# Order and form of the opening work of a two-layer encoder kernel: input halves, first weights, filter layers and filter maximum

## What is computed

```python
for layer in range(2):
    x = x + 0.5 * swiglu(rms_norm(x, ffn1_norm[layer]), wg, wu, wd)      # D_FF = 2816
    h = rms_norm(x, mix_norm[layer])
    x = x + (hyena_attention_mixer(h, ...) if layer == 0 else rwkv7_bidir_mixer(h, ...))
    x = x + 0.5 * swiglu(rms_norm(x, ffn2_norm[layer]), wg2, wu2, wd2)

# hyena_filter(L), which depends on weights alone, not on x:
hf = sin(freq * (z @ f1_w + f1_b))        # z: 256 x 33, layers of 64
hf = sin(freq * (hf @ f2_w + f2_b))
hf = sin(freq * (hf @ f3_w + f3_b))
hf = hf @ f4_w                            # 64 -> 2 x 512
h_f, h_b = hf[:, :512] * window, hf[:, 512:] * window
filt = concat(h_f[:1] + h_b[:1], h_f[1:], 0, h_b[:0:-1]);  filt /= sum(|filt|)
```

## Time and profile before

| | |
|---|---|
| median of 3 executions | 1247.82 us (1247.22 to 1248.85) |
| the profiled execution, device time | 1250.58 us |
| span of its trace, first to last instruction | 1248.8 us |
| PE busy | 1204.4 us (96%) |
| DVE, ACT, POOL busy | 804.6 us (64%), 657.7 us (53%), 404.7 us (32%) |
| chain of work that ended last | PE 81%, DVE 10%, ACT 6% |
| mean granted clock of PE | 0.986 |

### The profile page before, as it was taken

The page is one execution under the profiler, slowest core; times in us unless marked ns, Lnnn a source line. Parts: engine busy times, 40 slices in busy tenths (PEclk is TensorE's granted clock), DMA queues, the critical chain, the costliest instruction groups (busy, mean ns, idle before and its releaser), DMA issues.

```text
span 1248.8 us, 27159 instructions
## 1 busy us (share of the span) xinstructions
PE 1204.4 (96%) x11086; PEld 1086.2 (87%) x11086; DVE 804.6 (64%) x1280; ACT 657.7 (53%) x1118; POOL 404.7 (32%) x218
## 2 busy tenths in 40 slices
PE   8999999988999999999999989997999999999998
PEld 5899999876989999989999979986999888899998
DVE  7655555787685555485555479758777757755554
ACT  5545444664275445474454446665666544654552
POOL 0343443321123443323434410015343412334433
PEclk9999999998999999999999989988999999999999
DMA  9355445422255445554554534411000015554552
GB/s 359 110 194 202 171 182 202 152 102 102 101 205 200 167 185 202 195 199 175 189 201 166 194 146 152 152 51 53 4 4 4 3 59 198 203 193 166 195 190 96
DMA packets 18657, 187.99 MB, mean 151 GB/s; under 512 B 2065, under 2 KB 2577, under 8 KB 3601
## 3 DMA queue, kind: packets, MB, share of 16 engines
q1 hardware_dynamic: 18576, 186.84, 41.2%
HBM read 185.78 MB, written 1.05 MB: 150 GB/s over the span
## 4 chain that ended last, share of the span: by engine, by line
PE 81%; DVE 10%; ACT 6%; issue 1%; POOL 0%; DMA 0%; SPq 0%; DVEq 0%
PE gu_bank L265 24%; PE gu_bank L267 12%; PE bank L244 7%; PE bank L246 7%; PE bank L245 7%; PE bank L1446 7%; PE gu_bank L244 3%; PE gu_bank L1446 3%; PE gu_bank L246 3%; PE gu_bank L245 3%; DVE WL L199 2%; ACT WH L187 2%; PE gu_bank L1477 2%; DVE HX L395 1%; ACT WH L193 1%
## 5 line engine op out<-in xcount | busy, mean ns | idle before, releaser
L208 POOL TENSOR_TENSOR WL<-raw,WH 128x1024 fp32r<-128x1024 f32 x96 | 328.0, 3416 | 595.5 <-ACT WH L193 573.7
L265 PE MATMUL gu_bank<-HX,WH 128*128 128x512 f32 x1408 | 504.0, 400 | 6.4 <-DVE PL L531 4.5
L267 PE MATMUL gu_bank<-HX,WL 128*128 128x256 f32 x1408 | 396.0, 281 | 0.0
L199 DVE TENSOR_TENSOR WL<-raw,WH 128x2048 fp32r<-128x2048 f32 (+1 forms) x114 | 245.1, 2150 | 130.3 <-ACT WH L187 130.3
L265 PEld LDWEIGHTS gu_bank<-HX,WH 128*128 128x128 f32 x1408 | 265.4, 188 | 70.3 <-DVE PL L531 5.1
L267 PEld LDWEIGHTS gu_bank<-HX,WL 128*128 128x128 f32 x1408 | 266.8, 190 | 0.2
L187 ACT ACTIVATE WH<-raw 128x2048 fp32r<-128x2048 f32 (+1 forms) x114 | 205.0, 1799 | 26.5 <-PE gu_bank L246 14.4
L244 PE MATMUL bank<-PH,WH 128*128 128x256 f32 (+1 forms) x720 | 201.7, 284 | 1.0 <-ACT arena L2043 0.9
L245 PE MATMUL bank<-PL,WH 128*128 128x256 f32 (+1 forms) x720 | 201.6, 283 | 0.0
L246 PE MATMUL bank<-PH,WL 128*128 128x256 f32 (+1 forms) x720 | 201.5, 283 | 0.0
L452 ACT ACTIVATE work<-gu_bank 128x512 f32<-128x512 f32 x88 | 52.5, 597 | 168.3 <-PE gu_bank L267 168.3
(11 more groups left out here) (313 smaller groups left out, 1811.5 us busy)
## 6 DMA issues: line engine op xcount, KB each, us to landing
raw<-stream_in SPq DMA_DIRECT2D x114, 1536.0 KB, 6.5
cst<-const_in SPq DMA_DIRECT2D x1, 1568.0 KB, 17.8
X<-xT_in SPq DMA_DIRECT2D x1, 1024.0 KB, 6.1
raw<-stream_in SPq DMA_DIRECT2D x1, 1024.0 KB, 8.1
arena<-hconst_in SPq DMA_DIRECT2D x2, 512.0 KB, 11.4
out<-X SPq DMA_DIRECT2D x4, 256.0 KB, 2.1
arena<-hconst_in SPq DMA_DIRECT2D x1, 768.0 KB, 14.5
arena<-fw_in SPq DMA_DIRECT2D x1, 512.0 KB, 8.9
```

Of the source, the lines that this page charges most:

```text
L199: nc.vector.tensor_tensor(WL[:, slot, :cut], raw[:, slot, :cut], WH[:, slot, :cut].bitcast(fp32), ALU.subtract).then_inc(lo_ready, 1)
L208: (eng or nc.gpsimd).tensor_tensor(WL[:, slot, cut:end], raw[:, slot, cut:end], WH[:, slot, cut:end].bitcast(fp32), ALU.subtract).then_inc ...
L265: nc.tensor.matmul(out[:, :], WH[:, slot, w:w + P], HX[:, x, :, :].rearrange("p i t -> p (i t)"), start=k == 0, stop=False)
L267: return nc.tensor.matmul(out[:, L:2 * L], WL[:, slot, w:w + P], HH[:, x, :], start=False, stop=k == CT - 1)
```

## The change

- SP: x is loaded in two halves of four tiles with a semaphore each, the first weight step in its gate and its up block with a semaphore each; of step 1 only the two blocks in use are loaded; the ones matrix comes ahead of step 1; the load of step 2 is issued ahead of the two last constants.
- ACT (`act_opening`): four tiles of x, sine 0, four tiles, gate 0, up 0, squares, sine 1, and then weights 1 and sine 2 as before.
- DVE: each sine argument is formed in turns (frequency divided by 2 pi once, into `turn`), rounded and subtracted, three operations in place of seven; the sine's scale undoes the division. The order is argument 0, x tiles, weights 0, argument 1, weights 1 (gate and up, the latter taken from POOL), argument 2, sums of squares. The reciprocal root moves behind the even and odd part, and the filter's maximum ahead of the split of weights 2.
- PE: 4 and 3 fillers; the third filter layer behind block 0's up, gate 1 ahead of the filter output, and the statistics inside it, between its two halves.
- POOL: no split of step 1.

```diff
@@ -154,8 +154,10 @@
         blocks_done = sem("blocks_done")
-        par_full, feat_full, x_full, ones_full, fw_full, win_full, dft_full, rest_full = (
-            sem(f"{n}_full") for n in "par feat x ones fw win dft rest".split())
+        par_full, feat_full, ones_full, fw_full, win_full, dft_full, rest_full = (
+            sem(f"{n}_full") for n in "par feat ones fw win dft rest".split())
+        x_full = [sem("x_full0"), sem("x_full1")]
+        gate_full = sem("gate_full")
         down_first = sem("down_first")
@@ -211,9 +213,7 @@
             if s0 == 0:
-                pool.wait_ge(lo_ready, 2)
-                split_last(pool, s0 + 1, order=True)
-                split_last(pool, s0 + 2)
+                split_last(pool, s0 + 2, order=True)
             elif s0 != S_FFN[1]:
@@ -316,11 +316,11 @@
             project_both(0, bank[1], 0, 1).then_inc(blocks_done, 2)
+            pe_filter_layer(pe, 2)
+            pe.wait_ge(lo_ready, 2)
+            project_both(0, bank[2], 1, 0).then_inc(blocks_done, 1)
             pe.wait_ge(ones_full, 16)
             pe_filter_in(pe)
-            pe_stats(pe, 0)
-            pe.wait_ge(lo_ready, 2)
-            project_both(0, bank[2], 1, 0).then_inc(blocks_done, 1)
             pe.wait_ge(lo_last, 2)
@@ -373,14 +373,28 @@
-            if n == 0:
-                act.wait_ge(par_full, 16)
-                act.wait_ge(x_full, 16)
             for k in range(CT):
-                if n and k % 2 == 0:
+                if k % 2 == 0:
                     act.wait_ge(x_ready, 4 * (n - 1) + k // 2 + 1)
...
                     .then_inc(hh_ready, 1)
...
+        def act_opening(act, gain):
...
+            act.wait_ge(par_full, 16)
+            for j in range(2):
+                act.wait_ge(x_full[j], 16)
+                for k in range(HT * j, HT * j + HT):
+                    nc.scalar.activation(HH[:, k, :], X[:, k, :], ACT.Copy, scale=pcol(gain[0], gain[1] + k))\
+                        .then_inc(hh_ready, 1)
+                if j == 0:
+                    act_filter_sin(act, 0)
+            act.wait_ge(gate_full, 16)
+            nc.scalar.activation(WH[:, 0, :BLK], raw[:, 0, :BLK], ACT.Copy).then_inc(hi_ready, 1)
+            act.wait_ge(raw_full[0], 16)
+            split_hi_last(0, 0)
+            act_squares(act)
+            act_filter_sin(act, 1)
@@ -507,8 +521,9 @@
             next_lo(dve, s0 + 1)
-            if n:
-                split_last(dve, s0 + 1, eng=nc.vector, order=True)
+            split_last(dve, s0 + 1, eng=nc.vector, order=n > 0)
+            if n == 0:
+                dve_filter(dve, own, (2,))
             dve_sums(dve, own, n)
@@ -537,8 +552,8 @@
                 dve_filter_window(dve, Own(dve, flt_own), n)
+                dve_filter_max(dve)
                 next_lo(dve, s0 + 2)
-                dve_filter_max(dve)
             else:
@@ -627,6 +642,7 @@
         amax, anegm, asum, aes, aden, arden = (small[:, 4 + 2 * k:6 + 2 * k] for k in range(6))
+        turn = small[:, 59:60]
         ymix = prod
@@ -641,8 +657,7 @@
         ROUND = 1.5 * 2.0 ** 23
-        PI2 = [6.28125, float(np.float32(2 * math.pi - 6.28125))]
-        PI2.append(2 * math.pi - PI2[0] - PI2[1])
+        TURN = 6.283185
         SLOPES = [2.0 ** (-8.0 * (h + 1) / NQ) for h in range(NQ)]
@@ -709,16 +724,21 @@
                              start=True, stop=True).then_inc(flt_mm, 1)
-            for n in (1, 2):
-                pe_active((4, 7)[n - 1])
-                pe.wait_ge(flt_sin, n)
-                nc.tensor.matmul(b3[0:FO, 0:L], fw[0:FO, n * FO:(n + 1) * FO], FHID[0:FO, n - 1, :],
-                                 start=True, stop=True).then_inc(flt_mm, 1)
+            pe_active(4)
+            pe_filter_layer(pe, 1)
+            pe_active(3)
...
+        def pe_filter_layer(pe, n):
+            pe.wait_ge(flt_sin, n)
+            nc.tensor.matmul(bank[3][0:FO, 0:L], fw[0:FO, n * FO:(n + 1) * FO], FHID[0:FO, n - 1, :],
+                             start=True, stop=True).then_inc(flt_mm, 1)
...
             for a in range(2):
+                if a:
+                    pe_stats(pe, 0)
                 for i in range(2):
@@ -745,7 +765,7 @@
             act.wait_ge(flt_arg, n + 1)
-            nc.scalar.activation(FHID[0:FO, n, :], FARG[0:FO, 0, :], ACT.Sin).then_inc(flt_sin, 1)
+            nc.scalar.activation(FHID[0:FO, n, :], FARG[0:FO, 0, :], ACT.Sin, scale=-TURN).then_inc(flt_sin, 1)
@@ -764,16 +784,12 @@
                     dve.wait_ge(flt_sin, n)
-                own(ts(x, bank[3][0:FO, 0:L], pcol("f_b", n)[0:FO], pcol("freq")[0:FO], ALU.add, ALU.mult))
                 own.settle()
-                own(ts(k, x, INV2PI, ROUND, ALU.mult, ALU.add))
+                own(ts(x, bank[3][0:FO, 0:L], pcol("f_b", n)[0:FO], turn[0:FO], ALU.add, ALU.mult))
                 own.settle()
-                own(ts(k, k, -ROUND, None, ALU.add))
-                for c in PI2:
-                    own.settle()
-                    own(stt(out=x, in0=k, scalar=-c, in1=x, op0=ALU.mult, op1=ALU.add))
+                own(ts(k, x, ROUND, None, ALU.add))
                 own.settle()
-                ts(x, x, 3.1415925, -3.1415925, ALU.min, ALU.max).then_inc(flt_arg, 1)
+                stt(out=x, in0=k, scalar=-ROUND, in1=x, op0=ALU.add, op1=ALU.subtract).then_inc(flt_arg, 1)
@@ -781,14 +797,13 @@
                     own(nc.vector.tensor_tensor(HFB[:, i, a, :], DN[2 * a + i][:, :], window[:, a, :], ALU.mult))
...
-            dve_root(dve, n)
             own.settle()
...
             nc.vector.tensor_copy(HSD[0:1, 1, 0, :], HSD[0:1, 0, 0, :]).then_inc(flt_sum, 1)
+            dve_root(dve, n)
@@ -2447,20 +2462,26 @@
             fetch(fw[:, 0:3 * FO], fw_d[:, 0:3 * FO], feat_full)
-            fetch(X[:, :, :], xT, x_full)
-            sp.dma_start(raw[:, 0, 0:2 * BLK], stream[0, :, 0:2 * BLK]).then_inc(raw_full[0], 16)
+            for j in range(2):
+                fetch(X[:, HT * j:HT * j + HT, :], xT[:, HT * j:HT * j + HT, :], x_full[j])
+            sp.dma_start(raw[:, 0, 0:BLK], stream[0, :, 0:BLK]).then_inc(gate_full, 16)
+            sp.dma_start(raw[:, 0, BLK:2 * BLK], stream[0, :, BLK:2 * BLK]).then_inc(raw_full[0], 16)
+            fetch(cst[:, 0:P], const_d[:, 0:P], ones_full)
+            sp.dma_start(raw[:, 1, 0:2 * BLK], stream[1, :, 0:2 * BLK]).then_inc(raw_full[1], 16)
             fetch(fw[:, 3 * FO:NFW], fw_d[:, 3 * FO:NFW], fw_full)
             fetch(*hpart("window", HC["feat"]), win_full)
-            fetch(cst[:, 0:P], const_d[:, 0:P], ones_full)
-            sp.dma_start(raw[:, 1, :], stream[1]).then_inc(raw_full[1], 16)
             fetch(*hpart("cos", HC["icos"]), dft_full)
...
+            def load(s, u):
+                sp.dma_start(raw[:, u, :], stream[s]).then_inc(raw_full[u], 16)
...
+            sp.wait_ge(lo_ready, 1)
+            sp.wait_ge(lo_last, 1)
+            load(2, 0)
             fetch(*hpart("icos", HC["window"]), rest_full)
...
-            def load(s, u):
-                sp.dma_start(raw[:, u, :], stream[s]).then_inc(raw_full[u], 16)
...
-            for first, end in ((2, S_O + 1), (S_O + 3, STEPS)):
+            for first, end in ((3, S_O + 1), (S_O + 3, STEPS)):
                 if first == S_O + 3:
@@ -2502,11 +2523,7 @@
             nc.scalar.activation(small[:, 60:61], eps6[:, 0:1], ACT.Sin)
-            act_filter_sin(act, 0)
-            next_hi(act, 0)
-            act_filter_sin(act, 1)
-            act_norm_in(act, 0, ("ffn1_norm", 0))
-            act_squares(act)
+            act_opening(act, ("ffn1_norm", 0))
             act_ffn(act, 0, S_FFN[0], 0)
@@ -2543,11 +2560,12 @@
             dve.wait_ge(par_full, 16)
-            dve_filter(dve, own, (0, 1))
+            own(nc.vector.tensor_scalar(turn[0:FILTER_ORDER], pcol("freq")[0:FILTER_ORDER], INV2PI, None, ALU.mult))
+            dve_filter(dve, own, (0,))
+            dve_norm_in(dve, 0, ("ffn1_norm", 0))
             next_lo(dve, 0)
-            dve_norm_in(dve, 0, ("ffn1_norm", 0))
             split_last(dve, 0, eng=nc.vector)
-            dve_filter(dve, own, (2,))
+            dve_filter(dve, own, (1,))
             dve_ffn(dve, 0, S_FFN[0], 0, own)
```

## The result

| | before | after |
|---|---|---|
| median, us | 1247.83 (1243.27 to 1252.83, 20 executions) | 1251.83 (1246.29 to 1256.24, 20 executions) |
| profiled execution, us | 1250.58 | 1247.90 |
| span of its trace, us | 1248.8 | 1246.1 |

The changed kernel takes 1.0029 times as long (95% interval 1.0016 to 1.0042).

A forecast was written before the change was run, and what follows sets the result against it. PE sets the pace, but DVE's line with ACT pinches at step 3. Span 1248.8 - 1.0 (earlier step 3) + 1.5 (clock fall) = 1249.3, carried to the median as 1247.82 + 0.5 = 1248.3; range 1244.5 to 1250.5.

The forecast's parts named there:

- slower: Outcome for the whole kernel: slower by more than 0.2% (2.5 us), chance 0.12.
- POOL's split: After the statistics: POOL's split of step 2 starts at 29.5, inside DVE's addition, and its turn costs DVE 2.2 us.
- 0.6 us of delay: Input load: by an estimate from the skill page, two halves take about 0.6 us more than one whole.
- Rival C: Ahead of step 3: POOL does not stop DVE, step 3 starts at 48.4, no clock fall, 1244.6 us; chance 0.15.
- E: Opening: x's halves don't land apart or ACT's order delays the gate weights, 1.2 us later throughout, 1249.5; chance 0.08.
- D: Opening: PE's clock rises later, 1.5 us per extra low period, 1249.8, or 1251.3 from the second; chance 0.10.
- the +1.5 of the sum: Ahead of step 3: PE's new 2.8 us wait likely makes the clock fall, costing 1.5 us.
- step 3 starts 1.0 us earlier than before: PE's third weight step: starts at 50.6 instead of 51.64, the whole first-order gain.
- The old fall: Clock fall after 1.51 us idle at 26.80, worth 1.5 us on PE's own line; claimed to go.
- the diff touches nothing later: Behind the first 52 us: code from the third FFN weight step on is the same, so only the opening counts.
- the give-back: Ahead of the first gating product: the maximum before step 2's split gives back the 2.3 us gain, leaving 0.2 net.
- The 5.4 us of the prediction: DVE's line: the first gating product starts 5.4 us after the one-partition copy, where it was 3.26.

The follow-up runs named there:

- after_again: The changed kernel run once more with no edit: 1251.57 us, ratio 1.0034 to the kernel before.
- after_third: The changed kernel run again with no edit, side by side with padded ones, for a third trace: 1253.45 us, ratio 1.0033 to the kernel before.
- short_after: The changed kernel cut off behind its first FFN, mixers and later FFNs left out: 227.16 us.
- after_pad: The changed kernel with 39 repeated waits (20 do-nothing instructions) at PE's start: 1250.58 us, ratio 1.0019 to the kernel before.
- short_before: The kernel before, cut off behind its first FFN, mixers and later FFNs left out: 224.98 us.
- lo_first: The changed kernel with the split of step 2's weights put back ahead of the filter's maximum: 1251.52 us, ratio 1.0024 to the kernel before.
- short_pool_late: short_after with POOL's split of step 2 held until the filter's even and odd parts are done: 223.71 us.
- two_edits: The whole changed kernel with POOL's step 2 split held back and ACT's copy of step 1's sums ahead of its transform copies: 1248.09 us, ratio 0.9997 to before.

## Why the prediction was wrong

The forecast was 1248.3 with a range to 1250.5; the median of 1251.83 is 3.5 over it and out of the range, and "slower" had 0.12.

**Right within a us: the dates up to step 3.** In the trace of after: statistics 24.0 forecast, 23.98 measured; POOL's split 29.5, 29.54; both filter parts 33.8, 34.17; first gating product 39.2, 39.50; step 2 39.3, 39.63; step 3 50.6, 51.01; its wait 2.8, 2.58. In after_again and after_third the statistics are at 24.82 and 24.62 and step 3 at 51.85 and 51.65, so the closest of these agreements are also luck. That the halves of x land apart is in ACT's row of after:

```profile
6.77 1.70 ACT L388 ACTIVATE HX<-X,par 128x256 fp32r<-128x256 f32 x4 [4.53 <-DMA X<-xT_in]
...
10.28 1.04 ACT L393 ACTIVATE WH<-raw 128x1024 fp32r<-128x1024 f32 x1
```

The first tiles start at 6.77, where 7.0 was taken, and the gate block at 10.28, where ACT's own work put it at 10.6. In after_again and after_third the first tiles start at 7.61 and 7.41, and the gate block at 11.12 and 10.92, in both of them right behind ACT's own work. The prediction drew 0.6 us of delay from the page "DMA: Bandwidth & Descriptors" of the Trainium skill (Bandwidth, Measured), whose figures are for transfers issued from GpSimd: the trace of after doesn't have it, the two others have 0.6 and 0.4 over the 7.0 taken. The changed kernel loads x whole in no run, so what halving costs is not shown. PE was 1.39 us idle ahead of block 0, which was not forecast, and made it up by running sooner at the full clock (its six filler passes at 9.69 take 1.56 us, 0.26 each; the eight at 5.33 take 3.78, 0.47 each). Rival C is refuted by the 3.37 us of L802, and E doesn't occur. D, a later rise of the clock, doesn't occur in the three traces of the changed kernel, but it may have in short_after: from 12 to 16 us PE started 15 matmuls there and 19 in after, and its statistics stand at 25.19.

**Right in kind: the new wait costs a fall.** The nine matmuls and 1.5 us of short_after are the +1.5 of the sum. Of the seven whole kernels' traces with this wait one, after_pad, has the fall there, over 7 us:

```profile
51.00:58.00 7.00, 6.31 (x20) 5.41 (x21) 4.69 (x6) 3.51 (x4) 3.78 (x2) 0.51 0.43 145
```

The three traces of the changed kernel itself don't have it, though all wait 2.58 us. In the short kernel the clock's means say that all five executions had a fall; how usual it is in the whole kernel stays open.

**First step that failed: "step 3 starts 1.0 us earlier than before".** The base was one trace, the latest of three (51.64; the others have 51.04 and 51.49), and the changed kernel's step 3, forecast at 50.6, came at 51.01, 51.65 and 51.85, with x landing late in two of the three. On these means the gain of 1.0 is -0.1. The old fall came in at most three of five executions of short_before; the prediction treated it as always there. With a gain of nothing and a loss of 1.5 the opening comes to +1.5, and the cut-off kernels measured 1.8, give or take 0.9. The term was mis-sized by about one us.

**Second: "the diff touches nothing later".** This is the larger error, 2.3 to 2.8 us of the 4, each give or take more than one. The source behind step 3 is the same, but its place in PE's program isn't, and the padded kernels show that on the changed kernel the place alone has a price of that size. 1.8 and 2.3 to 2.8 make 4.1 to 4.6; measured are 4.2. With such intervals the close agreement is partly luck.

**Third: the place of the give-back.** The prediction put it on the maximum ahead of the split. lo_first shows that this order is worth 0.5 us of it: with the reciprocal moved behind the copy, the line from copy to first gating product has the reciprocal (1.73), the maximum (1.23) and the split (2.29) in it in any order. The 5.4 us of the prediction stand (33.76 + 0.41 to 39.50 is 5.33); what the change added to this line is the reciprocal, which stood ahead of the filter's parts before. What makes DVE's line long is POOL's turn, 3.5 us with the fall that hangs on it (short_pool_late).

**The range** had no term for the place in PE's program and none for the baseline's own spread, so its upper end was 1250.5, short of the result by 1.3.

## What to carry to other kernels

Before PE's work is moved forward, look at which line ends last at the next weight step: a gain on PE ahead of a pinch on another engine becomes an idle stretch, and, as behind the 2.58 us here, the clock may fall on top. Where DVE and POOL collide on the line that ends last, try making POOL wait until DVE's critical operations are done; in the short kernel that gained 3.5 us where this change lost 1.8. A date read from one trace of each kernel is a draw: here the start of step 3 moves by 0.8 us with the landing of the input. A change that alters the number of instructions on an engine should be timed with a few do-nothing instructions added, and over many executions, before 2 us in 1248 are put down to its content.

## What the runs showed of the hardware

- Four instructions that do nothing at PE's start change a kernel of 1250 us by 2.8 us, give or take 1.4, and a close relative of it (two_edits, with 4 or 20) by 0.5, give or take 1.5. Queue 8 carries instructions in packets of 16 KB (60 of them, 0.98 MB, in after), and the moment at which one runs beside a given load moves with such an edit.
- After 2.58 us of idle time the clock fell in short_after and after_pad, and not in six other traces; after 1.51 us it fell in all four traces of the kernel before, whole or short; near an idle stretch of 1.95 to 2.13 us at 553 to 561 us it fell in five of six traces, and near one of 1.44 to 1.75 us in none of nine. A fall cost 1.5 us, and one of 7 us in after_pad about the double, an estimate from its 20 matmuls in 7 us.
- DVE and POOL took turns at 29.5 us as they had at the earlier trace rows: 2.1 us on one DVE operation with two SBUF inputs, and nothing when POOL started behind it.
